# Streaming encoder layer on one core: gated activations held in PSUM until they are split, and up-weight sums placed between the down accumulations

## Chip, core and metric

The kernel runs on one core of a Trainium2 chip. The metric is the device time of one launch in microseconds (us), as the median of several runs. Engines are named as in the profile: PE is TensorE's matmul, PEld its weight load, DVE VectorE, ACT ScalarE, POOL GpSimd, SP the engine that issues the loads.

## What is computed

One layer of a hybrid encoder: an input projection, a pooling mixer beside grouped-query attention, an output projection with a residual, and a gated feed-forward block over 2048 + 64 rows of 1024 channels, with 2816 hidden channels. The change touches the last block alone:

```python
h = x + jnp.concatenate([pool_o, attn_o], axis=-1) @ w_out
hn = rms_norm(h, norm_ffn)
return h + (jax.nn.silu(hn @ w_gate) * (hn @ w_up)) @ w_down
```

## The kernel before

The rows go through the kernel in three parts (`Shape`, p = 0, 1, 2) of 768, 768 and 576 rows; the last part ends in the 64 sample rows. Each part runs projection, attention, output projection and then the feed-forward block, so there are three feed-forward stages.

**Precision.** Each fp32 operand is split into a high and a low fp32r half. `split_products` (L787) then makes three matmuls of one product (hi x hi, hi x lo, lo x hi: L790 to L792). ACT writes the high halves (`high_product`, L1226), POOL or DVE subtracts to get the low halves (POOL: L637).

**A feed-forward stage** is a loop over 11 groups of 256 hidden channels (j = 0 to 10). A group has a gate half (which = 0) and an up half (which = 1). Each half is a 2x2 block product made with seven block products instead of eight: `product` (L1052) issues them in the order 1, 6, 5, 7, 2, 3, 4 (`ORDER`). One product is 12 matmuls of 384 columns (288 in the third part). Between the two halves PE runs `down` of the group before (L1090), which multiplies its activations with `w_down`, tile by tile, and DVE adds each result to `h` (L1660). So PE's order in group j is: gate half of j, down of j-1, up half of j.

**Weight sums.** Products 5, 6 and 7 use sums of weight blocks, product 3 a further one. DVE makes them: `weight_sum(s, j, which, n)`, n = 1 to 4 (L1910, L1913, L1915, L1919). A ring of 4 slots holds the split weights: product q + 4 is split once product q is done.

**Block sums.** The seven products land in four PSUM banks: product 1 and 2 in bank 4, 6 in bank 5, 5 and 3 in bank 6, 7 and 4 in bank 7 (banks 0, 1, 2, 3 and 7 in group 0). `first_partial` (ACT, L1455) copies product 1 to `u2`, and DVE's `sums` combines: U2 (L1935), t (L1938), C22 (L1941), C12 (L1943), C21 (L1945). Gate sums go to `sg` in SBUF, up sums to `cc` and `u2` in SBUF. Product 4 accumulates onto product 7's bank, so PE waits for `c22_done` before it; a bank is written anew once the sum that read it is done.

**Activation.** ACT takes SiLU of the gate blocks (L1469). `gated` (DVE, L1963) multiplies an up block onto `sg`. ACT's `act_high` (L1476) rounds the result to `act_hi`, and DVE's `act_low` (L1975, and L1973 for the sample rows) subtracts to get `act_lo`. In the third part one `act_low` is three instructions. The last block's `act_high` and `act_low` run in the next group. `down_low` (DVE, L2019) makes the low half of the second `w_down` block, at the end of the group.

Every engine runs its instructions in written order and waits on semaphores, so what stands behind a waiting instruction waits too. DVE's order is the function `group` (L1979), ACT's the function `group` at L1479.

## Time and profile before

| what | value |
|---|---|
| median of 3 runs | 2350.99 us (2348.12 to 2352.45) |
| the profiled execution's own time | 2353.13 us |
| its span | 2351.3 us |
| PE busy | 2162.0 us, 92% |
| PEld busy | 1913.4 us, 81% |
| DVE busy | 1521.3 us, 65% |
| ACT busy, POOL busy | 939.1 us, 40%; 959.4 us, 41% |
| mean granted TensorE clock | 0.983 |
| chain that ended last | PE 59%, DVE 24%, issue 10%, ACT 6% |
| DMA | 160.04 MB, mean 68 GB/s |

The profile records one execution, whose own time lies 2.1 us above the median of the runs. Busy time of PE is modelled: a matmul's record is longer than the distance to the next one, since matmuls overlap. Distances between starts tell what one costs. The feed-forward stages run from about 285 to 808 us, 1101 to 1624 us and 1873 to 2331 us of the span.

### The profile page before, as it was taken

How to read it: one execution, taken by the hardware profiler on the slowest of the kernel's cores; microseconds unless marked ns; L12 is line 12 of the kernel's file. 1: busy time of each engine (PE TensorE's matmuls, PEld its weight loads, DVE VectorE, ACT ScalarE, POOL GpSimd, SP SyncE). 2: the span in 40 equal slices, each digit the busy share in tenths (PEclk: the TensorE clock that was granted, in tenths of full speed). 3: DMA queues.
4: the chain of work that ended last, by engine and by line, in shares of the span. 5: the costliest groups of instructions: out<-in, count | busy, mean ns of one | idle time of the engine just before them, and what ended most of it. 6: DMA issues, size and time to landing. Idle time of an engine off the chain costs nothing.

```text
span 2351.3 us, 34387 instructions
## 1 busy us (share of the span) xinstructions
PE 2162.0 (92%) x11991; PEld 1913.4 (81%) x11991; DVE 1521.3 (65%) x2375; ACT 939.1 (40%) x2070; POOL 959.4 (41%) x626
## 2 busy tenths in 40 slices
PE   7999899999999999998999999999998889898997
PEld 7876799988899788667999889988975678787886
DVE  4558665666666545675667665666458777777776
ACT  4666333332233346644333322324466333333331
POOL 2312354544454323123555434542311555555452
PEclk9999999999999999999999999999999999999999
DMA  4120022221122241110222212222411122222121
GB/s 132 45 71 29 11 90 68 68 80 54 54 71 67 87 143 55 54 37 19 72 72 73 70 54 62 68 67 83 143 33 58 40 90 81 80 71 84 58 81 50
DMA packets 194387, 160.04 MB, mean 68 GB/s; under 512 B 7005, under 2 KB 176906, under 8 KB 194282
## 3 DMA queue, kind: packets, MB, share of 16 engines
q1 hardware_dynamic: 191326, 149.58, 20.9%
q10 hardware_dynamic: 2956, 9.08, 1.1%
q8 instruction: 64, 1.05, 0.2%
q14 instruction: 41, 0.34, 0.0%
HBM read 149.66 MB, written 9.07 MB: 68 GB/s over the span
## 4 chain that ended last, share of the span: by engine, by line
PE 59%; DVE 24%; issue 10%; ACT 6%; DMA 0%; DVEq 0%; POOL 0%; SPq 0%; ACTq 0%
PE ps L790 18%; PE ps L791 18%; PE ps L792 18%; DVE act_lo L1975 5%; DVE s_sb L1819 2%; DVE negmax L1824 2%; ACT s_sb L1360 2%; DVE raw L1915 2%; DVE st L1910 2%; DVE sg L1963 1%; PE ps L804 1%; PE ps L897 1%; DVE h L1660 1%; DVE st L1919 1%; PE ps L935 1%
## 5 line engine op out<-in xcount | busy, mean ns | idle before, releaser
L637 POOL TENSOR_TENSOR ring_lo<-raw,ring_hi 128x512 fp32r<-128x512 f32 (+1 forms) x276 | 425.4, 1548 | 657.9 <-ACT ring_hi L1226 588.7
L1660 DVE TENSOR_TENSOR h<-ps,h 128x512 f32<-128x512 f32 (+1 forms) x476 | 325.4, 689 | 246.9 <-PE ps L792 237.2
L790 PE MATMUL ps<-xt_hi,ring_hi 128*128 128x384 f32 (+1 forms) x1152 | 380.1, 330 | 28.5 <-POOL ring_lo L637 24.4
L791 PE MATMUL ps<-xt_lo,ring_hi 128*128 128x384 f32 (+1 forms) x1152 | 376.3, 327 | 0.0
L792 PE MATMUL ps<-xt_hi,ring_lo 128*128 128x384 f32 (+1 forms) x1152 | 375.9, 326 | 0.0
L637 POOL TENSOR_TENSOR ring_lo<-st,ring_hi 128x512 fp32r<-128x512 f32 x198 | 265.3, 1347 | 178.5 <-ACT ring_hi L1226 178.1
L790 PE MATMUL ps<-tx,ring_hi 128*128 128x384 f32 (+1 forms) x792 | 259.6, 328 | 66.9 <-DVE sg L1941 61.2
L637 POOL TENSOR_TENSOR w_lo<-raw,w_hi 128x1024 fp32r<-128x1024 f32 x66 | 167.7, 2542 | 318.7 <-ACT w_hi L1203 318.6
L790 PE MATMUL ps<-w_hi,act_hi 128*128 128x512 f32 x704 | 284.3, 404 | 12.4 <-DVE act_lo L1975 9.9
L791 PE MATMUL ps<-w_lo,act_hi 128*128 128x512 f32 x704 | 282.7, 402 | 0.0
L792 PE MATMUL ps<-w_hi,act_lo 128*128 128x512 f32 x704 | 282.6, 401 | 0.0
L792 PE MATMUL ps<-tx,ring_lo 128*128 128x384 f32 (+1 forms) x792 | 256.8, 324 | 0.0
L791 PE MATMUL ps<-tx,ring_hi 128*128 128x384 f32 (+1 forms) x792 | 256.8, 324 | 0.0
L1455 ACT ACTIVATE uu<-ps 128x384 f32<-128x384 f32 (+1 forms) x66 | 30.7, 465 | 561.7 <-PE ps L792 498.1
L790 PEld LDWEIGHTS ps<-xt_hi,ring_hi 128*128 128x128 f32 x1152 | 218.7, 190 | 36.0 <-POOL ring_lo L637 16.1
L791 PEld LDWEIGHTS ps<-xt_lo,ring_hi 128*128 128x128 f32 x1152 | 218.7, 190 | 1.4
L792 PEld LDWEIGHTS ps<-xt_hi,ring_lo 128*128 128x128 f32 x1152 | 218.6, 190 | 0.0
L790 PEld LDWEIGHTS ps<-tx,ring_hi 128*128 128x128 f32 x792 | 150.1, 189 | 77.0 <-issue 69.3
L1226 ACT ACTIVATE ring_hi<-raw 128x512 fp32r<-128x512 f32 x264 | 162.3, 626 | 98.3 <-PE ps L792 96.2
L1226 ACT ACTIVATE ring_hi<-st 128x512 fp32r<-128x512 f32 x198 | 124.2, 629 | 163.2 <-DVE st L1919 88.6
L790 PEld LDWEIGHTS ps<-w_hi,act_hi 128*128 128x128 f32 x704 | 135.7, 193 | 45.2 <-issue 12.4
L792 PEld LDWEIGHTS ps<-w_hi,act_lo 128*128 128x128 f32 x704 | 134.9, 192 | 33.2
(206 smaller groups left out, 4225.0 us busy)
## 6 DMA issues: line engine op xcount, KB each, us to landing
raw<-in_w_gate SPq DMA_DIRECT2D x66, 512.0 KB, 4.4
raw<-in_w_up SPq DMA_DIRECT2D x66, 512.0 KB, 4.0
raw<-in_w_down SPq DMA_DIRECT2D x66, 512.0 KB, 3.3
raw<-in_w_in SPq DMA_DIRECT2D x33, 512.0 KB, 4.0
raw<-in_w_out SPq DMA_DIRECT2D x24, 512.0 KB, 4.4
h<-in_x_prompt SPq DMA_DIRECT2D x16, 512.0 KB, 6.9
out<-h ACTq DMA_DIRECT2D x16, 512.0 KB, 2.8
xload<-in_x_prompt SPq DMA_DIRECT2D x10, 512.0 KB, 6.0
```

The costliest lines, as they stand in the source:

```text
L637: nc.gpsimd.tensor_tensor(lo, raw, hi.bitcast(F32), ALU.subtract).then_inc(done, 1)
L790: nc.tensor.matmul(out, w_hi, m_hi, start=first, stop=False, skip_group_check=onto)
L791: nc.tensor.matmul(out, w_hi, m_lo, start=False, stop=False, skip_group_check=onto)
L792: return nc.tensor.matmul(out, w_lo, m_hi, start=False, stop=last, skip_group_check=onto)
L1226: nc.scalar.activation(ring_hi[:, slot], left(which, p), ACT.Copy).then_inc(hi_done, 1)
L1360: nc.scalar.activation(p, p, ACT.Exp, bias=negmax[0:rows, ai % 2, hh:hh + 1], accum_out=den[0:rows, ai % 2, hh:hh + 1])
L1660: nc.vector.tensor_tensor(out, ps[0:rows, bank, :], out, ALU.add).then_inc(d_free, 1)
L1819: last = nc.vector.scalar_tensor_tensor(s_sb[0:rows, b, hh, c0:c1], dist[0:rows, c0:c1], SLOPES[GQA * g + hh], ps[0:rows, 4 + e, 256 * j + ...
L1824: link(nc.vector.tensor_reduce(negmax[0:rows, b, :], s_sb[0:rows, b, :, c0:c1], AX.X, ALU.max, negate=True))
L1910: nc.vector.tensor_tensor(first, b[:, 0:HALF], b[:, HALF:], ALU.add).then_inc(s_ready, 1)
L1915: nc.vector.tensor_tensor(b[:, 0:HALF], a[:, 0:HALF], b[:, 0:HALF], ALU.subtract)\
L1975: last = nc.vector.tensor_tensor(act_lo[:, c, dst], sg[:, b, src], act_hi[:, c, dst].bitcast(F32), ALU.subtract)
```

## The change

Four things change; the number of compute instructions stays.

- **Where the up sums and the product live.** The up half's C22, C12 and C21 are written back to PSUM: C22 to the bank of U2's product, C12 and C21 to the bank that they read. `gated` multiplies in place in PSUM, by `sg` from SBUF. `act_high` and `act_low` read PSUM. `a_bank` names the banks.
- **Who waits for that.** PE's first gate product of the next group waits for `al_done` of the second block where it waited for `a_done`; products 5 and 7 of the gate half get a wait for the third and the fourth block's `al_done`. `first_partial` of the gate half no longer waits for the last `gated`.
- **DVE's order.** The four up sums of weights leave the place between t and C22 of the gate half: n = 1 goes behind C21, n = 2 and 3 behind the first tile's accumulation, n = 4 behind the third tile's. The sums of the next gate half move up by one tile. `down_low` of j-1 moves from the end of group j-1 to between t and C22 of the gate half of j. The last `act_low` goes from the next group to the end of its own.
- **ACT's order.** The last `act_high` goes from the next group to its own, ahead of the second `w_down` rounding (L1502).

```diff
+        def a_bank(j, block):
+            first = isinstance(j, int) and j == 0
+            b = BLOCKS.index(block)
+            return ps[:, ((2, 1, 3, 7) if first else (5, 4, 6, 7))[b]]
...
                 if p == 1 and not first:
                     if which == 0:
-                        pe.wait_ge(a_done, s.g0 + 4 * j - 2)
+                        pe.wait_ge(al_done, s.g0 + 4 * j - 2)
...
                 elif p == 5:
                     need(pe, c12_done, m)
+                    if which == 0 and not first:
+                        pe.wait_ge(al_done, s.g0 + 4 * j - 1)
                 elif p == 7:
                     need(pe, c21_done, m)
+                    if which == 0 and not first:
+                        pe.wait_ge(al_done, s.g0 + 4 * j)
...
                     if s and prev and 1 <= t <= s.nt:
+                        if t == 1:
+                            pe.wait_ge(al_done, prev.g0 + 4 * GROUPS)
                         norm_transposes(s, t - 1)
...
-                if which == 0:
-                    need(act, a_done, s.g0 + 4 * j)
-                else:
-                    act.wait_ge(c21_done, m)
+                need(act, c21_done, m)
...
-                    need(act, al_done, s.g0 + 4 * j - 2)
+                    need(act, a_done, s.g0 + 4 * j - 2)
...
-                    last = nc.scalar.activation(act_hi[:, c, dst], sg[:, b, src], ACT.Copy)
+                    last = nc.scalar.activation(act_hi[:, c, dst], a_bank(j, block)[:, src], ACT.Copy)
...
-                    if n == 0:
-                        act_high(s, j - 1, (1, 0))
+                    if p == 4 and which == 1:
+                        act_high(s, j, (1, 0))
...
-                out = cc[:, 0:s.NB] if which else sg[:, BLOCKS.index(block), 0:s.NB]
+                out = sg[:, BLOCKS.index(block), 0:s.NB]
+                if which:
+                    out = cc[:, 0:s.NB] if part in ("U2", "t") else a_bank(j, block)[:, 0:s.NB]
+                t_tile = cc[:, 0:s.NB] if which else out
...
-                g = sg[:, b, 0:s.NB]
-                nc.vector.tensor_tensor(g, up, g, ALU.mult).then_inc(a_done, 1)
+                up = a_bank(j, block)[:, 0:s.NB]
+                nc.vector.tensor_tensor(up, up, sg[:, b, 0:s.NB], ALU.mult).then_inc(a_done, 1)
...
-                    last = nc.vector.tensor_tensor(act_lo[:, c, dst], sg[:, b, src],
+                    last = nc.vector.tensor_tensor(act_lo[:, c, dst], a_bank(j, block)[:, src],
                                                    act_hi[:, c, dst].bitcast(F32), ALU.subtract)
...
                 weight_sum(s, j, 0, 4)
-                if not first:
-                    act_low(s, j - 1, (1, 0))
                 sums(s, j, 0, "U2")
                 sums(s, j, 0, "t")
-                for n in (1, 2, 3):
-                    weight_sum(s, j, 1, n)
+                if first:
+                    for n in (1, 2, 3):
+                        weight_sum(s, j, 1, n)
+                else:
+                    down_low(s, j - 1)
                 for part in ("C22", "C12", "C21"):
                     sums(s, j, 0, part)
+                if not first:
+                    weight_sum(s, j, 1, 1)
+                between = {0: () if first else ((1, 2), (1, 3)), 1: ((0, 1),), 2: ((0, 2), (1, 4)), 3: ((0, 3),)}
                 for t in range(s.nt):
                     if not first:
                         accumulate_tile(s, OUT_GROUPS + j - 1, odd, t, t)
-                    if 1 <= t <= 3 and not last:
-                        weight_sum(s, j + 1, 0, t)
-                weight_sum(s, j, 1, 4)
+                    for which, n in between.get(t, ()):
+                        if which == 1:
+                            weight_sum(s, j, 1, n)
+                        elif not last:
+                            weight_sum(s, j + 1, 0, n)
...
                 act_low(s, j, (0, 1))
-                if last:
-                    act_low(s, j, (1, 0))
-                else:
-                    down_low(s, j)
+                act_low(s, j, (1, 0))
```

DVE at the start of a group (j = 9 of the first part, whose instructions stand unrolled), before: the last weight sum of the gate half (L1919), the `act_low` that was left over, U2, t, three up sums of weights, then the three block sums.

```order
L1919 TENSOR_TENSOR st<-raw,st 128x512 [waits split2]
L1975 TENSOR_TENSOR act_lo<-sg,act_hi 128x384 [waits ah_done]
L1935 TENSOR_TENSOR uu<-ps,uu 128x384 [waits u1_done,prod_done]
L1938 TENSOR_TENSOR sg<-ps,uu 128x384 [waits u2_done,prod_done]
L1910 TENSOR_TENSOR st<-raw 128x512 [waits split2,raw2_loaded3,raw2_loaded2]
L1913 TENSOR_TENSOR st<-st,raw 128x512 [waits s_ready]
L1915 TENSOR_TENSOR raw<-raw 128x512
L1941 TENSOR_TENSOR sg<-ps,sg 128x384 [waits t_done,prod_done]
L1943 TENSOR_TENSOR sg<-ps,uu 128x384 [waits prod_done]
L1945 TENSOR_TENSOR sg<-ps,uu 128x384 [waits prod_done]
L1660 TENSOR_TENSOR h<-ps,h 128x512 [waits d_ready] x4
```

The same place in the changed kernel (its lines stand 6 to 12 lower in the file: L1928 is L1919 before, L2028 is L2019, L1953 is L1941, L1669 is L1660).

```order
L1928 TENSOR_TENSOR st<-raw,st 128x512 [waits split2]
L1947 TENSOR_TENSOR uu<-ps,uu 128x384 [waits u1_done,prod_done]
L1950 TENSOR_TENSOR sg<-ps,uu 128x384 [waits u2_done,prod_done]
L2028 TENSOR_TENSOR w_lo<-raw,w_hi 128x1024 [waits hi_done]
L1953 TENSOR_TENSOR sg<-ps,sg 128x384 [waits t_done,prod_done]
L1955 TENSOR_TENSOR sg<-ps,uu 128x384 [waits prod_done]
L1957 TENSOR_TENSOR sg<-ps,uu 128x384 [waits prod_done]
L1919 TENSOR_TENSOR st<-raw 128x512 [waits split2,raw2_loaded3,raw2_loaded2]
L1669 TENSOR_TENSOR h<-ps,h 128x512 [waits d_ready] x2
L1922 TENSOR_TENSOR st<-st,raw 128x512 [waits s_ready]
L1924 TENSOR_TENSOR raw<-raw 128x512
L1669 TENSOR_TENSOR h<-ps,h 128x512 [waits d_ready] x2
```

Between t and C22 one instruction now stands where three stood, and the three up sums stand behind C21 and the first tile.

DVE at the end of the same group, from the up half's C22 on, before, up to the first instruction of the next group:

```order
L1941 TENSOR_TENSOR uu<-ps,uu 128x384 [waits t_done,prod_done]
L1963 TENSOR_TENSOR sg<-uu,sg 128x384 [waits c22_done,silu_done]
L1963 TENSOR_TENSOR sg<-ps,sg 128x384 [waits prod_done,silu_done]
L1975 TENSOR_TENSOR act_lo<-sg,act_hi 128x384 [waits ah_done]
L1943 TENSOR_TENSOR uu<-ps,uu 128x384 [waits prod_done]
L1963 TENSOR_TENSOR sg<-uu,sg 128x384 [waits c12_done,silu_done]
L1975 TENSOR_TENSOR act_lo<-sg,act_hi 128x384 [waits ah_done]
L1945 TENSOR_TENSOR uu<-ps,uu 128x384 [waits prod_done]
L1963 TENSOR_TENSOR sg<-uu,sg 128x384 [waits c21_done,silu_done]
L1975 TENSOR_TENSOR act_lo<-sg,act_hi 128x384 [waits ah_done]
L2019 TENSOR_TENSOR w_lo<-raw,w_hi 128x1024 [waits hi_done]
L1919 TENSOR_TENSOR st<-raw,st 128x512 [waits split2]
```

In the changed kernel:

```order
L1953 TENSOR_TENSOR ps<-ps,uu 128x384 [waits t_done,prod_done]
L1969 TENSOR_TENSOR ps<-ps,sg 128x384 [waits c22_done,silu_done]
L1969 TENSOR_TENSOR ps<-ps,sg 128x384 [waits prod_done,silu_done]
L1981 TENSOR_TENSOR act_lo<-ps,act_hi 128x384 [waits ah_done]
L1955 TENSOR_TENSOR ps<-ps,uu 128x384 [waits prod_done]
L1969 TENSOR_TENSOR ps<-ps,sg 128x384 [waits c12_done,silu_done]
L1981 TENSOR_TENSOR act_lo<-ps,act_hi 128x384 [waits ah_done]
L1957 TENSOR_TENSOR ps<-ps,uu 128x384 [waits prod_done]
L1969 TENSOR_TENSOR ps<-ps,sg 128x384 [waits c21_done,silu_done]
L1981 TENSOR_TENSOR act_lo<-ps,act_hi 128x384 [waits ah_done] x2
L1928 TENSOR_TENSOR st<-raw,st 128x512 [waits split2]
```

Every instruction but the last now reads or writes PSUM for the activations, `w_lo` is gone from the end, and a fourth `act_lo` stands there.

## Rows read from the trace of the kernel before

**Rows 1.** PE's waits: who waited for what, us in total, times, longest.

```profile
PE ps L790 <- DVE sg L1941: 61.2, 31, 2.5
PE ps L790 <- POOL ring_lo L637: 24.4, 24, 1.5
...
PE ps L790 <- DVE act_lo L1975: 9.9, 3, 4.4
```

**Rows 2.** Windows of one group: bounds, length, busy per engine, PEclk, DMA share, GB/s.

```profile
478.06:526.35 48.29, 46.53 (x240) 42.93 (x241) 30.93 (x40) 14.56 (x27) 22.70 (x15) 1.00 0.22 65
1964.40:2007.40 43.00, 37.89 (x225) 33.98 (x225) 31.43 (x48) 14.13 (x31) 22.16 (x15) 0.96 0.24 74
2007.40:2048.85 41.45, 36.35 (x224) 32.70 (x225) 31.39 (x48) 14.04 (x31) 22.18 (x15) 1.00 0.25 76
```

**Rows 3.** Timeline of PE, first part: start, length, instruction, [idle before <- releaser].

```profile
524.08 0.34 PE L791 MATMUL ps<-xt_lo,ring_hi 128*128 128x384 f32 x1
524.25 0.34 PE L792 MATMUL ps<-xt_hi,ring_lo 128*128 128x384 f32 x1
526.35 0.41 PE L790 MATMUL ps<-tx,ring_hi 128*128 128x384 f32 x1 [1.77 <-DVE sg L1941]
...
560.07 0.34 PE L790 MATMUL ps<-xt_hi,ring_hi 128*128 128x384 f32 x1
```

**Rows 4.** Timeline of DVE, same gate half.

```profile
521.27 1.08 DVE L1910 TENSOR_TENSOR st<-raw 128x512 f32<-128x512 f32 x1
...
523.98 1.76 DVE L1915 TENSOR_TENSOR raw<-raw 128x512 f32<-128x512 f32 x1
525.66 0.54 DVE L1941 TENSOR_TENSOR sg<-ps,sg 128x384 f32<-128x384 f32 x1
```

**Rows 5.** Timeline of POOL, the same gate half and the up half behind it.

```profile
521.76 3.43 POOL L637 TENSOR_TENSOR ring_lo<-raw,ring_hi 128x512 fp32r<-128x512 f32 x2
...
558.98 1.59 POOL L637 TENSOR_TENSOR ring_lo<-st,ring_hi 128x512 fp32r<-128x512 f32 x1 [0.73 <-ACT ring_hi L1226]
```

**Rows 6.** By line: instructions, ns min/median/max, first and last start, forms.

```profile
L1935 DVE TENSOR_TENSOR uu<-ps,uu x66: 443/547/558, 297.7 to 2318.8; 128x384 f32<-128x384 f32 x44, 128x288 f32<-128x288 f32 x22
L1963 DVE TENSOR_TENSOR sg<-uu,sg x99: 458/559/2548, 313.1 to 2329.8; 128x384 f32<-128x384 f32 x66, 128x288 f32<-128x288 f32 x33
L2019 DVE TENSOR_TENSOR w_lo<-raw,w_hi x33: 1217/2307/2310, 323.6 to 2326.7; 128x1024 fp32r<-128x1024 f32 x33
```

**Rows 7.** Timeline of DVE, end of an up half.

```profile
558.19 0.56 DVE L1943 TENSOR_TENSOR uu<-ps,uu 128x384 f32<-128x384 f32 x1 [1.09 <-PE ps L792]
558.85 0.56 DVE L1963 TENSOR_TENSOR sg<-uu,sg 128x384 f32<-128x384 f32 x1
559.33 1.66 DVE L1975 TENSOR_TENSOR act_lo<-sg,act_hi 128x384 fp32r<-128x384 f32 x1
```

**Rows 8.** Timeline of PE, a gate half of the third part.

```profile
1991.81 0.30 PE L790 MATMUL ps<-xt_hi,ring_hi 128*128 128x288 f32 x1
1991.94 0.29 PE L791 MATMUL ps<-xt_lo,ring_hi 128*128 128x288 f32 x1
...
1997.18 0.37 PE L790 MATMUL ps<-tx,ring_hi 128*128 128x288 f32 x1 [0.44 <-DVE uu L1945]
...
2000.53 0.39 PE L790 MATMUL ps<-xt_hi,ring_hi 128*128 128x288 f32 x1 [1.52 <-POOL ring_lo L637]
...
2003.03 0.40 PE L790 MATMUL ps<-xt_hi,ring_hi 128*128 128x288 f32 x1 [0.65 <-POOL ring_lo L637]
...
2007.39 0.37 PE L790 MATMUL ps<-tx,ring_hi 128*128 128x288 f32 x1 [2.50 <-DVE sg L1941]
```

**Rows 9.** Timeline of DVE, the same place.

```profile
1992.75 2.63 DVE L1975 TENSOR_TENSOR act_lo<-sg,act_hi 128x256 fp32r<-128x256 f32 x1
```

**Rows 10.** Timeline of ACT, the same place.

```profile
1997.63 0.41 ACT L1455 ACTIVATE uu<-ps 128x288 f32<-128x288 f32 x1 [2.77 <-DVE sg L1963]
```

**Rows 11.** Timeline of PE behind a wait in the first part's last group.

```profile
719.95 0.52 PE L791 MATMUL ps<-tx,ring_hi 128*128 128x384 f32 x1
```

More of the change, by code:

```diff
@@ L1505, in group @@
                         silu(s, j, block)
-                    elif block and (p != 4 or last):
+                    elif block and p != 4:
                         act_high(s, j, block)
@@ L1940, in sums @@
                     dve.wait_ge(t_done, m + 1)
-                    nc.vector.tensor_tensor(out, b4, out, ALU.add).then_inc(c22_done, 1)
+                    nc.vector.tensor_tensor(out, b4, t_tile, ALU.add).then_inc(c22_done, 1)
                 elif part == "C12":
@@ L1944, in sums @@
                 else:
-                    nc.vector.tensor_tensor(two if which else out, b4, two, ALU.add).then_inc(c21_done, 1)
+                    nc.vector.tensor_tensor(out, b4, two, ALU.add).then_inc(c21_done, 1)
             def gated(s, j, block):
-                first = isinstance(j, int) and j == 0
                 m, b = s.m0 + 2 * j + 1, BLOCKS.index(block)
@@ L1954, in gated @@
                     dve.wait_ge(prod_done, s.q0 + seq(j, 1, 2) + 1)
[L1955 to L1963 removed]
+                else:
+                    dve.wait_ge({(1, 1): c22_done, (0, 1): c12_done, (1, 0): c21_done}[block], m + 1)
+                up = a_bank(j, block)[:, 0:s.NB]
+                nc.vector.tensor_tensor(up, up, sg[:, b, 0:s.NB], ALU.mult).then_inc(a_done, 1)
             def act_low(s, j, block):
```

10 lines of the change are left out of this document (2 added, 8 removed).

## The prediction

> **What bounds the kernel now.** I read the waits of PE first, since PE is busy for 92% of the span. One wait outweighs all others: product 4's first matmul waits for C22 of the gate half, 31 times, 61.2 us together; behind it come 24 waits for POOL's low halves, 24.4 us [rows 1]. Then the windows of single groups: in the first two parts a group takes 48.3 us, in the third 41.5 us, or 43.0 us where the granted clock reads 0.96 [rows 2]. So the thing to read is one group, and what PE waits for in it.
>
> In the first two parts PE's matmuls of a product start 0.17 us apart; before product 4 of the gate half 2.10 us pass between two starts [rows 3]. That costs 1.93 us, once in each of groups 1 to 10. DVE shows why: product 7 is long done, but three up sums of weights stand between t and C22, from 521.27 to 525.66, 4.4 us [rows 4]. Two of them are slow: 1.08 and 1.76 us. POOL is in its own subtractions just then, two of them in 3.43 us [rows 5]. C22 ends at 526.20 and PE starts at 526.35: 0.15 us from the end of a DVE instruction to the matmul that waits for it.
>
> In the third part four waits stand in one gate half: 0.44 us for C21 of the up half before, 1.52 and 0.65 us for POOL's low halves, 2.50 us for C22 [rows 8]. Starts are 0.13 us apart and a record is 0.30 us, so each wait costs its idle time plus 0.17 us: 5.11 + 0.68 = 5.8 us per group, in ten groups. The cause lies before them: `act_low` of an up block takes 2.63 us [rows 9], the last `gated` comes late behind it, and ACT's `first_partial` waits 2.77 us for that [rows 10]. ACT's rounding of product 2's weights stands behind `first_partial`, and POOL's low half behind that.
>
> **DVE's slow instructions.** The record shows when they are slow. A sum with one operand in PSUM and one in SBUF never exceeds 558 ns over 66 instructions, in the same stretches in which POOL works. `gated` with both operands in SBUF has the same median, 559 ns, but reaches 2548 ns; the `w_down` subtraction takes 1217 ns at least and 2307 ns in the median [rows 6]. The `act_low` of 1.66 us [rows 7] starts 0.35 us after a POOL subtraction of 1.59 us [rows 5].
>
> **The change, part by part.**
>
> *Up sums out of the gate half.* The three sums, 4.4 us, leave the stretch between t and C22. `down_low` takes their place. It is unhidden only if it delays C22. Its ends are 1.22 and 2.31 us [rows 6]; I take the upper, since POOL has four subtractions to make there. Count from gate product 1's start (time 0), a product being 2.1 us: U2 can start at about 4.3, t at 6.4, `down_low` ends by 9.3. C22 needs product 7, done at 8.4, so it ends at about 9.8; product 4 begins at 12.6. There are 2.8 us to spare and the wait goes. Saving: 1.93 us x 20 groups = 38.6 us in the first two parts. Below zero this cannot fall, unless something else becomes late (next items).
>
> *Where the sums go.* Behind C21 and between the down accumulations. DVE is busy for 30.9 of 48.3 us [rows 2], and its idle time lies mostly between the accumulations of `down`, whose 16.9 us (13.1 in the third part; a group less its 14 products and waits) need no new ring slot. Four sums of 0.7 us (1.8 if POOL interferes) are 2.8 to 7.2 us; the accumulations may fall behind by one unit, since PE runs four banks ahead. ACT is held before the split of product 6's weights until sum 2 is done, 3.4 to 5 us into `down`; three splits and POOL's three low halves (1.3 to 1.6 us each) end 9 to 10 us into it. PE wants them at 13.1 at the earliest. I cost this at zero; what covers it is `down`.
>
> *Activations in PSUM.* No operand pair lies in SBUF any more, so `gated` and `act_low` should take 0.56 us, or 0.46 in the third part [rows 6]. No row shows DVE writing PSUM. Its nearest rows are 0.56 us, the sums that read it, and 2.55 us, the worst of these places in SBUF; nothing suggests less than 0.56, as the element count is the same. I take 0.56, whose rows have the same operands. The gain is that C21 and the last `gated` come on time and that `first_partial` follows C21.
>
> *The new wait.* PE's first gate product now waits for `act_low` of the second block. The chain is: C12 at 558.19, `gated` at 558.85, `act_low` at 559.33 [rows 7]. At 0.56 us it ends at 559.89, plus 0.15 is 560.04; PE starts that product at 560.07 [rows 3]. It just fits: I allow 0.1 us x 20 = 2 us. In the third part C12 starts 1.4 us ahead of product 1's due start, `gated` 0.56 later, `act_low` 0.37 after that, and its three pieces end 0.6 us on: 0.15 us past the due start, with the 0.15 of the release 0.3 to 0.4 us a group. What queues behind it on PE is everything. Products 5 and 7 wait for blocks three and four, due at 1.9 and 2.8 us, when PE needs them at 4.2 and 6.3 (3.2 and 4.8 in the third part): nothing. ACT's last `act_high` goes ahead of one 1.05 us rounding and behind one `gated`; `first_partial` still comes at about 3 us instead of 3.6.
>
> The Trainium skill, "VectorE: DVE Perf Modes", section on the TRN2 errata, gives a PSUM source 62 cycles more fixed cost than an SBUF source. By it, as an estimate, two instructions of this chain would be 0.065 us longer each, and the sum 30 x 0.13 = 4 us higher. The medians of 547 and 559 ns [rows 6] show no such difference, so I leave it out.
>
> *Third part.* Without the late `gated`, product 2's low half is done at about 6.2 us, before PE needs it (6.8). Product 3's is tight: weight sum 4 and `down_low` alternate with POOL's subtractions, which puts it at 8.7, when PE wants it at 8.2: 0.4 us. Product 4's comes at 10.0, due at 10.4. So of 5.8 us some 0.8 stay: 5.0 x 10 = 50 us.
>
> *Ends of the parts.* The last `down` of each part waits for `act_low`, 9.9 us in the three, 4.4 us in the last [rows 1]. There `gated` of the first block waits out POOL's `w_down` subtraction, with up to 2.55 us [rows 6]. At 0.56 or 0.46 us it ends 1.5 to 2.1 us earlier, of which ACT's roundings and the products themselves let 1.0 to 2.0 through: 4 us together.
>
> *TensorE's clock.* Seven times in the loops the spacing is that of 1.2 GHz for some 3 us, a matmul reading 0.52 us [rows 11] against 0.34 [rows 3]; each time it begins within 1.4 us after a wait of 1.8 us or more. In the third part that is the difference of 43.00 and 41.45, 1.55 us [rows 2]; the seven cost 10.8 us. With no wait over 0.5 us left in the loops they should go; I take 9 us.
>
> **Sum:** 38.6 - 2 + 50 + 4 + 9 = 99.6 us. The profiled execution took 2353.1 us, which gives 2253.5; the median of the runs lies 2.1 us lower, so **2251 us**. All of the 38.6, 58 and 10.8 us and the 9.9 us of the part ends together would be 117 us, 2234: no time below that.
>
> **Rivals.**
>
> *POOL holds the third part.* The 1.52 and 0.65 us waits need not hang on `first_partial`. For it: POOL is busy 22.2 of 41.5 us [rows 2], nearly all of it in the two halves and the first of `down`. Against: it idles before product 2. If both stay, 2.5 us a group instead of 0.4 are 21 us: 2272. A DVE write to PSUM of 0.8 us instead of 0.56 adds 0.5 us at product 1, 30 times, up to 2287.
>
> *DVE stays slow.* If an instruction that writes PSUM still has to take turns with POOL, `act_low` of the second block ends at 560.99 as before [rows 7] and product 1 waits 1.1 us in 20 groups; in the third part it ends 4.8 us late. Then 20 x 0.8 + 10 x 1 us remain of the gains in the loops, with some clock: 2320.
>
> *Slower.* The wait at product 1 takes the place of that at product 4 and is longer. Place: DVE's `act_low` of block 2. POOL's `w_down` subtraction starts about 0.2 us after time 0; if `act_low` falls behind it, as its 2.63 us show [rows 9], it ends near 3.4 and PE waits 3.6 us in place of 1.93. The point from which it decides is 1.8 us past product 1's due start. 20 x 1.6 us = 32 us: 2383. Against: operands in PSUM have never waited for POOL.
>
> *No effect.* The savings in the gate half return as waits in the up half, because ACT stands behind weight sum 2. That needs it some 7 us later than worked out above: 2350.
>
> **Chances.** Forecast 0.66, own range 2238 to 2266; POOL or a dearer PSUM write 0.25, 2266 to 2290; DVE slow 0.04; slower 0.03; no effect 0.02. The range 2238 to 2288 leaves out under 2 in 10. About 0.2%, 5 us, is what can be told from no change here. Faster: 0.95; the same: 0.02; slower: 0.03.
>
> **What would show it.** Right: a group of 46.4 us in the first two parts and 36.5 in the third; no PE wait for C22; `gated` and `act_low` with a maximum near 560 ns; a small wait of PE for `act_lo` at product 1; no loop window with a clock under 0.99. Wrong: `act_lo` as PE's largest releaser with more than 0.5 us a time; POOL's low half before products 2 and 3 of the third part; DVE instructions `ps<-ps,sg` over 0.8 us.

## The result, and the profile after

The changed kernel takes **2237.9 us** in the median of four runs (2237.53 to 2238.54), the kernel before beside it 2351.7 us: ratio 0.9515, with a 95% interval of 0.9497 to 0.9533. The forecast was 2251 us with a range from 2238 to 2288; the result lies a tenth of a microsecond under the low end, some 13 us below the forecast.

| what | before | after |
|---|---|---|
| the profiled execution's own time | 2353.13 us | 2238.25 us |
| its span | 2351.3 us | 2236.4 us |
| PE busy | 92% | 95% |
| DVE busy | 1521.3 us, 65% | 1327.4 us, 59% |
| ACT, POOL busy | 939.1, 959.4 us | 938.4, 940.2 us |
| mean granted TensorE clock | 0.983 | 0.990 |
| chain that ended last | PE 59%, DVE 24%, issue 10% | PE 80%, DVE 11%, ACT 6% |

From the start of group 0's second product to the first matmul of the last `down`, a stage's length went as follows. Stages one and two: 522.8 to 499.8 us and 522.4 to 499.8 us, together 45.6 us less. Stage three: 457.5 to 392.4 us, 65.1 us less. Everything outside these stretches: 4.2 us less. The forecast's sum, sorted in the same way (its clock term by the places of the seven stretches, its part ends by part), had about 43, 57 and 0.

First PE's waits in the changed kernel, the answer to [rows 1]; columns are who waited for whom, us in total, times, longest.

```profile
PE ps L796 <- DVE act_lo L1981: 6.5, 5, 2.3
PE ps L796 <- POOL ring_lo L643: 3.1, 6, 0.9
...
PE ps L796 <- DVE sg L1953: 0.7, 1, 0.7
```

The 31 waits for C22 are down to one, in group 0 of the third part; the 24 for POOL's low halves to six. What is left for `act_lo` are the three ends of the parts and two short ones, at product 1 of the last two of the third part's ten groups; in the other eight PE is idle there for 0.07 us, too little to be counted. The windows of single groups, which answer to [rows 2], one of the first part and one of the third (bounds, length, busy of PE, PEld, DVE, ACT, POOL with counts, PEclk, DMA share, GB/s):

```profile
499.96:546.22 46.26, 46.26 (x242) 42.94 (x241) 25.89 (x39) 14.60 (x26) 21.85 (x16) 1.00 0.23 68
...
2052.69:2088.50 35.81, 35.74 (x225) 32.63 (x225) 24.28 (x49) 13.96 (x31) 22.05 (x16) 1.00 0.30 88
```

In the first part PE is busy for all of the 46.26 us: nothing but its own products is left. The third part is at 35.81 us with 0.07 us idle. DVE, which makes 2375 instructions in either kernel, is busy for 5.0 us less per group in the first part, and 7.1 us less in the third (31.39 before).

By line, the answer to [rows 6]: instructions, ns min/median/max, first and last start, forms.

```profile
L1953 DVE TENSOR_TENSOR ps<-ps,uu x33: 466/566/567, 315.5 to 2209.0; 128x384 f32<-128x384 f32 x22, 128x288 f32<-128x288 f32 x11
...
L1969 DVE TENSOR_TENSOR ps<-ps,sg x132: 456/567/567, 316.2 to 2214.8; 128x384 f32<-128x384 f32 x88, 128x288 f32<-128x288 f32 x44
...
L1981 DVE TENSOR_TENSOR act_lo<-ps,act_hi x176: 181/487/558, 318.2 to 2216.3; 128x384 fp32r<-128x384 f32 x88, 128x256 fp32r<-128x256 f32 x44, 128x32 fp32r<-128x32 f32 x44
...
L2028 DVE TENSOR_TENSOR w_lo<-raw,w_hi x33: 1215/1215/1434, 328.6 to 2211.6; 128x1024 fp32r<-128x1024 f32 x33
```

The maximum of `gated` fell from 2548 to 567 ns, that of `act_low` to 558. Here a write of 384 columns to PSUM costs 9 ns more than one to SBUF (567 against 558 ns). And `down_low`, priced at 2.31 us in the forecast, takes 1.2 us in its new place in the first two parts, 1.35 to 1.43 us in the third. Gate product 4 of the first part shows why it may now stand there, against [rows 3, 4]. DVE first, then PE; columns are start, length, instruction.

```profile
559.96 1.22 DVE L2028 TENSOR_TENSOR w_lo<-raw,w_hi 128x1024 fp32r<-128x1024 f32 x1
561.57 0.56 DVE L1953 TENSOR_TENSOR sg<-ps,sg 128x384 f32<-128x384 f32 x1 [0.40 <-PE ps L798]
```

```profile
565.43 0.34 PE L798 MATMUL ps<-xt_hi,ring_lo 128*128 128x384 f32 x1
565.61 0.34 PE L796 MATMUL ps<-tx,ring_hi 128*128 128x384 f32 x1
```

C22 ends at 562.12, 3.3 us before PE wants it, and starts are 0.18 us apart across the boundary. The new dependence at product 1, in the first part, against [rows 7]:

```profile
551.77 0.57 DVE L1969 TENSOR_TENSOR ps<-ps,sg 128x384 f32<-128x384 f32 x1
552.25 0.55 DVE L1981 TENSOR_TENSOR act_lo<-ps,act_hi 128x384 fp32r<-128x384 f32 x1
```

```profile
552.81 0.34 PE L798 MATMUL ps<-tx,ring_lo 128*128 128x384 f32 x1
552.99 0.34 PE L796 MATMUL ps<-xt_hi,ring_hi 128*128 128x384 f32 x1
```

`act_low` ends at 552.80, and PE starts at 552.99 without a gap. How near that is depends on the release: C22's end and the matmul that waits for it are 0.15 us apart [rows 3, 4], but where PE does wait for `act_low` at product 1, it starts 0.06 us after its end in the first eight of a part's ten groups and 0.15 us after it in the last two (the third part here, all parts in `e6_act_low_twice` below). So in this group, the sixth, the step has 0.14 us to spare; in the last two it has 0.05. In the third part the same step is late, and product 3 just so. DVE, PE and POOL of one group there:

```profile
2141.57 0.41 DVE L1981 TENSOR_TENSOR act_lo<-ps,act_hi 128x256 fp32r<-128x256 f32 x1
...
2147.75 1.35 DVE L2028 TENSOR_TENSOR w_lo<-raw,w_hi 128x1024 fp32r<-128x1024 f32 x1
```

```profile
2142.32 0.37 PE L796 MATMUL ps<-xt_hi,ring_hi 128*128 128x288 f32 x1 [0.16 <-DVE act_lo L1981]
...
2150.34 0.38 PE L796 MATMUL ps<-xt_hi,ring_hi 128*128 128x288 f32 x1
2150.55 0.30 PE L797 MATMUL ps<-xt_lo,ring_hi 128*128 128x288 f32 x1
```

```profile
2147.97 2.29 POOL L643 TENSOR_TENSOR ring_lo<-st,ring_hi 128x512 fp32r<-128x512 f32 x1
```

At product 1 the distances between starts are 0.40 us longer than they would be (0.32 before the first matmul, 0.08 before the second), at product 3 0.08 us (2150.34 to 2150.55 instead of 0.13). This is the ninth of the ten groups; in the seven before it, with the shorter release, product 1 costs 0.34 us (0.23 and 0.11) and product 3 0.15 us (0.04 and 0.11). The four waits of [rows 8] are gone, but for 0.58 and 0.48 us for POOL's low halves in the first of the ten. Note that an idle time under 0.1 us has no bracket in the timeline: the distance between starts is the surer reading.

### The profile page after: what moved, and what is told of

It is laid out like the page before. It is cut to its first block, busy times and chain, and to the rows that moved or that the text cites. A ratio compares the mean times of both kernels' runs of the same rounds, so it can differ in the third digit from the quotient of the medians.

```text
span 2236.4 us, 34415 instructions
## 1 busy us (share of the span) xinstructions
PE 2135.8 (95%) x11991; PEld 1900.1 (85%) x11991; DVE 1327.4 (59%) x2375; ACT 938.4 (42%) x2070; POOL 940.2 (42%) x626
## 3 DMA queue, kind: packets, MB, share of 16 engines
q8 instruction: 64, 1.05, 0.2%
## 4 chain that ended last, share of the span: by engine, by line
PE 80%; DVE 11%; ACT 6%; issue 2%; POOL 1%; DMA 1%; SPq 0%; DVEq 0%; ACTq 0%; POOLq 0%
PE ps L796 25%; PE ps L797 25%; PE ps L798 25%; DVE s_sb L1828 2%; DVE negmax L1833 2%; ACT s_sb L1372 2%; PE ps L810 1%; PE ps L903 1%; DVE h L1669 1%; PE ps L941 1%; DVE xt_lo L1876 1%; PE ps L919 1%; DVE kt_sb L1750 1%; ACT pt_sb L1389 1%; POOL ring_lo L643 1%
## 5 line engine op out<-in xcount | busy, mean ns | idle before, releaser
L643 POOL TENSOR_TENSOR ring_lo<-raw,ring_hi 128x512 fp32r<-128x512 f32 (+1 forms) x276 | 414.3, 1509 | 438.6 <-ACT ring_hi L1238 373.3
L1669 DVE TENSOR_TENSOR h<-ps,h 128x512 f32<-128x512 f32 (+1 forms) x476 | 322.0, 686 | 148.9 <-PE ps L798 145.1
L643 POOL TENSOR_TENSOR w_lo<-raw,w_hi 128x1024 fp32r<-128x1024 f32 x66 | 159.4, 2417 | 318.6 <-ACT w_hi L1215 318.6
L796 PE MATMUL ps<-tx,ring_hi 128*128 128x384 f32 (+1 forms) x792 | 254.6, 321 | 1.3 <-DVE sg L1953 0.7
L797 PE MATMUL ps<-tx,ring_hi 128*128 128x384 f32 (+1 forms) x792 | 254.3, 321 | 0.0
L797 PEld LDWEIGHTS ps<-w_lo,act_hi 128*128 128x128 f32 x704 | 133.0, 189 | 30.6
```

What stands on the lines that cost most here:

```text
L643: nc.gpsimd.tensor_tensor(lo, raw, hi.bitcast(F32), ALU.subtract).then_inc(done, 1)
L796: nc.tensor.matmul(out, w_hi, m_hi, start=first, stop=False, skip_group_check=onto)
L797: nc.tensor.matmul(out, w_hi, m_lo, start=False, stop=False, skip_group_check=onto)
L1669: nc.vector.tensor_tensor(out, ps[0:rows, bank, :], out, ALU.add).then_inc(d_free, 1)
```

## The experiments

The table gives the length of a group in the steady stretch of each kind of part, and the median.

| kernel | parts 1 and 2 | part 3 | median, us |
|---|---|---|---|
| before | 48.29 | 41.45 | 2351.7 |
| new order alone | 46.30 | 38.29 | 2274.4 |
| PSUM alone | 46.91 | 37.33 | 2266.9 |
| changed, but product in SBUF | 47.04 | 40.37 | 2293.4 |
| changed, `down_low` at the end | 46.27 | 36.24 | 2245.5 |
| changed | 46.26 | 35.81 | 2237.9 |

### Each half of the change alone

`e1_psum_alone` keeps the activations in PSUM and goes back to DVE's order of before, but for the last `act_low`, which stays at the end of its own group:

```diff
-                else:
-                    down_low(s, j - 1)
...
+                for n in (1, 2, 3):
+                    weight_sum(s, j, 1, n)
...
+                if not last:
+                    down_low(s, j)
```

> The changed kernel with the weight sums and the w_down subtraction back in their old places; only the activations stay in PSUM (and the last act_low stays at the end of its group). Theory A (each half of the change is enough for the wait at product 4 in the first two parts): with gated and act_low at 0.56 us, DVE reaches t about 3.3 us earlier than before, the three sums still stand ahead of C22, but C22 ends at about 11.1 us after gate product 1's start where PE needs it at 12.4: no wait, a group of 46.3 us. In the third part PE needs it at 9.9 and a wait of about 1 us stays: 37 us a group, 2250 us in all. Theory B (as the prediction had it: the place of the sums makes the wait at product 4): the wait of 1.8 us stays in most of the 20 groups and that of 2.5 us in the third part's ten, 20 x 1.9 + 10 x 2.7 = 65 us over the changed kernel, 2303 us.

Measured: 2266.9 us (ratio 0.9639, 0.9623 to 0.9656), between the two. Theory A was right for the third part (37.33 us a group, 37 expected) and wrong for the first two (46.91 us in place of 46.3); Theory B put the wait three to five times too long. The waits of PE, and DVE's gate half in this kernel:

```profile
PE ps L796 <- DVE sg L1953: 16.9, 31, 0.8
```

```profile
518.75 1.53 DVE L1919 TENSOR_TENSOR st<-raw 128x512 f32<-128x512 f32 x1
520.32 1.67 DVE L1922 TENSOR_TENSOR st<-st,raw 128x512 f32<-128x512 f32 x1
521.91 1.77 DVE L1924 TENSOR_TENSOR raw<-raw 128x512 f32<-128x512 f32 x1
523.61 0.54 DVE L1953 TENSOR_TENSOR sg<-ps,sg 128x384 f32<-128x384 f32 x1
```

The wait for C22 is back at all 31 places, but with 0.4 us in the first part and 0.83 us in the third, not 1.77 and 2.50. The three sums are as slow as ever (4.9 us from the first one's start to C22's, 4.4 before); the gate half's work merely begins earlier. The prediction put the wait at product 4 down to the place of the sums alone, but 1.38 of its 2.0 us in the first parts go without touching that place.

`e2_order_alone` is the kernel before with the new places of DVE's sums and of `down_low` and nothing else; its last `act_low` still runs in the next group:

```diff
-                for n in (1, 2, 3):
-                    weight_sum(s, j, 1, n)
+                if first:
+                    for n in (1, 2, 3):
+                        weight_sum(s, j, 1, n)
+                else:
+                    down_low(s, j - 1)
```

> The kernel before with the new order of DVE alone: sums between the down accumulations, w_down's subtraction between t and C22; activations in SBUF as before. Both theories: the wait for C22 goes in all three parts. Theory A and B alike give 46.3 us a group in the first two parts. In the third part the waits for C21 (0.44 us) and for POOL's low halves (1.52 and 0.65 us), which I put down to the late gated and act_low, stay: about 3 us a group, 39 us a group, low-clock stretches fewer than before: 2275 us. If the POOL waits came from the sums instead, this kernel would reach the changed one's 35.8 us a group and 2245 us.

Measured: 2274.4 us (0.9672, 0.9651 to 0.9693). In parts one and two the order alone does the whole thing, 1.99 of 2.02 us a group. In the third it leaves 2.5 us a group (L1938 is the sum t, L1945 C21):

```profile
PE ps L790 <- POOL ring_lo L637: 11.4, 13, 1.0
PE ps L790 <- DVE sg L1938: 11.1, 10, 1.8
...
PE ps L790 <- DVE uu L1945: 5.7, 10, 1.9
```

The wait for t is new. It stands at product 3, where the kernel before waited for POOL's low half, and is 11.1 us in the ten groups; the forecast of 2275 us was met with this wait in the place of one of POOL's that it had named.

So the two halves, order and PSUM, save 77 and 85 us alone and 114 together. They overlap: each shortens the same queue of DVE in front of the same matmuls, and what one has freed the other can't free again.

### What matters about PSUM

`e3_product_in_sbuf` is the changed kernel whose `gated` writes the product to SBUF; ACT's rounding and `act_low` read it there. ACT's SiLU of the next gate half, which writes the same buffer, must then wait for `act_low`. The line that matters most:

```diff
-                nc.vector.tensor_tensor(up, up, sg[:, b, 0:s.NB], ALU.mult).then_inc(a_done, 1)
+                nc.vector.tensor_tensor(sg[:, b, 0:s.NB], up, sg[:, b, 0:s.NB], ALU.mult).then_inc(a_done, 1)
```

> The changed kernel, but gated writes its product to sg in SBUF, and act_high and act_low read it there; the up sums stay in PSUM, PE's waits stay as changed. Theory L (an instruction of DVE with both operands in SBUF takes turns with POOL, one with an operand in PSUM doesn't): gated stays at 0.56 us, act_low reads up to 1.6 to 2.6 us again, PE waits for the second block's act_low 1.1 us in each of 20 groups and 3.5 to 4.8 us in each of the third part's ten: 2295 to 2310 us. Theory W (what made gated and act_low slow before was their late start behind the sums, not their operands): act_low stays near 0.56 us and the time within 5 us of the changed kernel's 2238.

Measured: 2293.4 us (0.9752, 0.9731 to 0.9772), just under the range of Theory L and 50 us from Theory W: product 1 comes 0.77 us late in the first two parts, where 1.1 was expected. `gated` stays fast (one input in PSUM, 558 ns); `act_low`, both inputs now in SBUF, has a mean of 1221 ns for the shape that took 551. The third part shows it at its plainest, on DVE, POOL and PE:

```profile
1985.80 1.41 DVE L1981 TENSOR_TENSOR act_lo<-sg,act_hi 128x256 fp32r<-128x256 f32 x1
1987.13 2.32 DVE L1979 TENSOR_TENSOR act_hi<-sg,act_hi 128x32 fp32r<-128x32 f32 x1
```

```profile
1986.89 2.52 POOL L643 TENSOR_TENSOR w_lo<-raw,w_hi 128x1024 fp32r<-128x1024 f32 x1
```

```profile
1989.62 0.40 PE L796 MATMUL ps<-xt_hi,ring_hi 128*128 128x288 f32 x1 [3.21 <-DVE act_lo L1981]
```

An instruction over 32 columns, 0.18 us elsewhere, takes 2.32 us and ends at 1989.45, when POOL's subtraction ends (1989.41). This is the mechanism that the rival "slower" had put at this place, with 3.6 us of waiting: 3.21 us were measured once the input lay in SBUF. The Trainium skill, "SBUF — State Buffer", section "Who interferes with whom", says that a DVE instruction with two SBUF inputs contends with a GpSimd instruction that reads SBUF and that one with at most one, outside the two-port modes, does not. All rows above agree: of the 132 `gated` and 176 `act_low` of the changed kernel none exceeds 567 ns.

### What `down_low` is worth in the gate half

`e4_down_low_at_end` moves it back to the end of the group.

```diff
-                else:
-                    down_low(s, j - 1)
...
+                if not last:
+                    down_low(s, j)
```

> The changed kernel with the w_down subtraction of DVE back at the end of its group instead of between t and C22. If its place matters (as the prediction cost it, 2.3 us in turns with POOL there, and 0.4 us of wait at product 3 in the third part), the third part gets 0.3 us a group faster or, as it now meets POOL's 2.4 us w_down subtraction, U2 and t come 1 us later, still ahead of PE. My theory: DVE has 2.8 us to spare in the gate half either way, the time stays within 3 us of 2238. The rival, that this place was needed: waits of PE for u2 or t, over 0.3 us a group, 2247 us or more.

Measured: 2245.5 us (0.9543, 0.9527 to 0.9559). The forecast of this run, no more than 3 us, was wrong: the third part's group is 36.24 us, 0.43 us longer, and the whole third stage 3.4 us. PE's timeline of one such group has it at product 7:

```profile
2010.68 0.40 PE L796 MATMUL ps<-tx,ring_hi 128*128 128x288 f32 x1 [0.16 <-POOL ring_lo L643]
```

The start before it is at 2010.22, so that product 7 comes 0.33 us late and its second matmul another 0.10. Product 2 is 0.14 us late too, while product 3, 0.15 us late in the changed kernel, is on time. Of the 8.8 us between the two profiled runs 3.4 are these; 2.4 lie ahead of the first stage and 3.0 between the first two, where the granted clock shows more stretches at 1.2 GHz (at 238, 269 and 1061 us) than in the changed kernel's profile. Nothing was changed there, so they are not put down to the move.

`e7_down_low_twice` makes the subtraction twice where the change has put it.

```diff
+                if not last:
+                    nc.vector.tensor_tensor(w1_lo[:, 1], raw1[:, 1], w1_hi[:, 1].bitcast(F32), ALU.subtract)\
+                        .then_inc(dose, 1)
+                    dve.wait_ge(dose, (GROUPS - 1) * s.p + j + 1)
```

> The changed kernel with down_low's subtraction made twice in the gate half (1.2 to 1.35 us, with a 0.1 us turn between). It tests the step of the prediction that gave product 3 of the third part 0.4 us of waiting behind POOL. Theory: POOL's low half for product 3 ends at the moment PE wants it (2150.26 against 2150.34 plus the release), and with one more two-input subtraction in SBUF on DVE it ends about 1.2 us later, in ten groups: 12 us, 2250 (2246 to 2253); the first two parts keep 46.27 us, since C22 has 3.3 us there. Rival: POOL is not held by DVE but only DVE by POOL, and nothing changes in the third part either: 2238 to 2240.

Measured: 2248.8 us (2243.9 to 2250.2; 0.9555, 0.9541 to 0.957). Parts one and two keep 46.27 us. The third part's group is 36.42 us, 0.61 longer, half of what was expected, and at another product. That the median falls into the expected 2246 to 2253 us is luck: the profiled run took 2243.9 us, 5.6 us over the changed kernel, and the longer times of the others are not in what the profile shows.

```profile
2078.66 1.43 DVE L2030 TENSOR_TENSOR w_lo<-raw,w_hi 128x1024 fp32r<-128x1024 f32 x1
2080.12 2.20 DVE L2033 TENSOR_TENSOR w_lo<-raw,w_hi 128x1024 fp32r<-128x1024 f32 x1
```

```profile
2078.97 2.27 POOL L644 TENSOR_TENSOR ring_lo<-st,ring_hi 128x512 fp32r<-128x512 f32 x1
2081.20 3.51 POOL L644 TENSOR_TENSOR ring_lo<-raw,ring_hi 128x512 fp32r<-128x512 f32 x2
```

```profile
2083.51 0.40 PE L797 MATMUL ps<-tx,ring_hi 128*128 128x288 f32 x1 [0.36 <-POOL ring_lo L644]
```

In these rows DVE and POOL take turns instruction by instruction, each ending 1.1 to 1.2 us after the other. The low half of product 3 pays for the first copy only; the second copy delays the one of product 4 by about that much. Product 4 starts 0.52 us late, so it had some 0.6 us to spare.

### How tight product 1 is

`e6_act_low_twice` puts one more subtraction ahead of the `act_low` for which product 1 waits.

```diff
+                if b == 1:
+                    src, dst = s.pieces(nb)[0]
+                    nc.vector.tensor_tensor(cc[:, src], a_bank(j, block)[:, src],
+                                            act_hi[:, c, dst].bitcast(F32), ALU.subtract)
```

> The changed kernel with one more subtraction of the same size into a scratch buffer just ahead of act_low of block (0,0), the one that PE's first gate product waits for. My theory: in the first two parts act_low ends just as PE gets there (552.80 plus 0.15, PE at 552.99), so the 0.47 us of one more instruction show as 0.43 us in 20 groups, and in the third part, which already waits, as 0.33 us in 10 groups: 12 us more, 2250 (2247 to 2254). Rival: there is slack that the profile does not show (the wait is covered by PE's queue), and only the third part pays: 2241.

Measured: 2247.4 us (2242.0 to 2252.4; 0.9544, 0.9525 to 0.9563). A group takes 46.69 us in the first two parts, 0.43 more, and 36.02 in the third, 0.21 more. PE at product 1 of the first part:

```profile
556.32 0.34 PE L798 MATMUL ps<-tx,ring_lo 128*128 128x384 f32 x1
556.82 0.44 PE L796 MATMUL ps<-xt_hi,ring_hi 128*128 128x384 f32 x1 [0.16 <-DVE act_lo L1985]
557.10 0.34 PE L797 MATMUL ps<-xt_lo,ring_hi 128*128 128x384 f32 x1
```

The 0.43 us are those worked out, but by luck. The first start is late by 0.33 us only, and the second by another 0.11, which the working left out; `act_low` ends 0.06 us ahead of PE's start, not 0.15, in all but the last two groups of a part. So of the 0.46 us that `act_low` comes later 0.33 show, and the slack in these groups is 0.14 us: little, but more than the 0.04 that a release of 0.15 us gives. In the third part product 1 pays the expected 0.33 us, and the 0.12 us that product 3 lost before are gone behind it.

### What sends the clock down

`e8_wait_dose` brings the wait at product 4 back by repeated sums whose result goes to a scratch buffer, 7, 9 and 11 of them in the three parts.

```diff
+                        for i in range(n):
+                            nc.vector.tensor_tensor(cc[:, 0:s.NB], b4, t_tile, ALU.add).then_inc(dose, 1)
+                            dve.wait_ge(dose, base + i + 1)
```

> The changed kernel with sums repeated into a scratch buffer ahead of C22 of the gate half, so that PE waits before product 4 again in groups 1 to 10: 7 sums in the first part, 9 in the second, 11 in the third, which by the trace (C22's end at 562.12, product 4 at 565.6; 0.66 us a repeated sum, 0.56 in the third part) makes the wait about 1.35, 2.7 and 3.7 us. It tests what sends the clock to 1.2 GHz. Theory: the low stretches follow waits of about 1.8 us or more, so none in the loops of the first part, some (2 to 5) in the second, most groups in the third, about 1.6 us each: 77.5 us of waits and 8 to 20 us of clock, 2323 to 2336. Rival: the stretches come by chance and have nothing to do with the waits: 2315, and no more low stretches than the changed kernel has.

Measured: 2312.6 us (2307.1 to 2316.2; 0.983, 0.9815 to 0.9845). The repeated sums came out shorter than assumed. PE's product 4 in the three parts:

```profile
569.66 0.41 PE L798 MATMUL ps<-tx,ring_hi 128*128 128x384 f32 x1 [0.64 <-DVE sg L1961]
...
1276.84 0.41 PE L798 MATMUL ps<-tx,ring_hi 128*128 128x384 f32 x1 [1.83 <-DVE sg L1961]
...
2055.89 0.37 PE L798 MATMUL ps<-tx,ring_hi 128*128 128x288 f32 x1 [2.85 <-DVE sg L1961]
```

The idle times are the same to 0.01 us in the groups of a part, 0.64, 1.83 and 2.85 us, but for the third part's first wait of 2.12 us. Behind them a stretch of 3.0 to 3.4 us in which starts lie as far apart as at 1.2 GHz follows after none of the ten in the first part, after four of the ten in the second (at 1131, 1278, 1425 and 1571 us), after seven of the nine long ones in the third. Each costs 1.5 to 1.7 us. The four of the second part come at every third group, 147 us apart. The time alone would not have told the theories apart, because the waits added 60 us, not 77; the count of stretches does: eleven where the changed kernel has none.

### Trying to go further

`e5_early_low` brings `act_low` of block (0, 0) ahead of the sum C12, and in the last group two of them ahead of C21.

```diff
+                else:
+                    act_low(s, j, (0, 0))
                 sums(s, j, 1, "C12")
```

> The changed kernel with act_low of the first block moved ahead of the sum C12 in all groups but the last, and in the last group act_low of the first two blocks ahead of the sum C21. My theory: DVE's order alone makes the 0.33 us at product 1 of the third part (ten groups, 3.3 us), since block (0,0) is rounded long before C12 and its low half only waits behind it, and about 1.5 us of the 2 us wait at each of the three part ends, because there the low halves stand behind C21: 7 to 8 us in all, so 2230 us (2228 to 2233), with the third part's group at 35.5 us instead of 35.82. Rival: act_low then delays C12 and the gated product of block (0,1) by its own half microsecond, ACT's rounding of it comes later, and the wait only moves to product 5 or to ACT: 2238, no change.

Measured: 2237.1 us (2232.5 to 2240.8), ratio 0.9504 (0.9489 to 0.9519): no gain, and the rival was right that the wait only moves, though not in where it goes. Product 1 starts without a gap, and the third part's group still takes 35.82 us:

```profile
2112.29 0.40 PE L796 MATMUL ps<-tx,ring_hi 128*128 128x288 f32 x1
...
2115.70 0.40 PE L796 MATMUL ps<-xt_hi,ring_hi 128*128 128x288 f32 x1
```

The starts before these are at 2112.04 and 2115.44, so that 0.12 us are lost at product 7 and 0.13 at product 3, and 0.11 more behind each. Both take their low half from POOL. At the ends of the parts little of the expected 4.5 us was gained. From the first matmul of the tenth `down` to the next stage's first product 59.7 us pass in the first part, as in the changed kernel: PE's wait for `act_lo` of 1.95 us is gone, but 1.05 us of waiting for C21 stand in its place, and the wait ahead of the next stage's first product grows from 1.90 to 2.50 us. In the second part the same stretch is 0.7 us shorter (58.8 to 58.1), and in the third, up to the last instruction, 0.8 us (44.7, against 45.5 in the profiles that have no stretch at 1.2 GHz there). What the first two parts' groups lose (46.30 in place of 46.27 us) takes 0.6 of it back.

That pointed to two chains of equal length in the third part, DVE's and POOL's. `e9_pool_late` shortens POOL's: its subtraction of the down weights goes behind product 4's low half.

```diff
+                        if n == 2 and order is not GROUP0:
+                            low1(DOWN_ID, first - 2)
                         if n in down_at:
                             number = number + 1
-                            if n == down_at[0]:
+                            if n == down_at[0] and last:
```

> The changed kernel with POOL's subtraction of the down weights (2.4 us) moved from ahead of the low half of gate product 7 to behind that of gate product 4, where POOL has time before the down products. It asks what holds the third part's group at 35.82 us, 0.4 us over what its products alone take, since the run with the early act_low left it at 35.82. Theory: two chains are equally long there, DVE's act_low in front of product 1 and POOL's low halves for products 7 to 3; taking POOL's alone away frees 0.1 us at product 3 and leaves the 0.33 at product 1: 35.7 us a group, 1 us in all, 2237. Rival: POOL alone is the bound, and the whole 0.4 us goes: 35.4, 2234. Second rival: the load of the next down weights waits for this subtraction and the next gate weights' load stands behind it on SP's queue; then the weight sums between the accumulations come late: 2240 or more.

`e10_pool_late_early_low` adds to it the early `act_low` in the third part (but its last group), and the changed kernel itself ran beside them.

> Both at once: POOL's subtraction of the down weights behind gate product 4's low half, and, in the third part but its last group, act_low of block (0,0) ahead of the sum C12. Theory of the two equally long chains: the third part's group falls to the products' own time, 35.4 us, no start of PE in the gate half over 0.1 us late: 9 x 0.4 = 3.6 us under the changed kernel, 2234. Rival (a third chain, ACT's, lies just behind): 35.7 to 35.8 us, 2237 to 2238.

> The changed kernel itself, beside the two others on the same chip, since they are expected only 1 to 4 us away from it: 2238 (2236 to 2240) by both theories.

Measured: 2235.4 us (2232.1 to 2236.4) with POOL's move alone, **2232.4 us** (2232.3 to 2236.3; ratio 0.949, 0.9477 to 0.9503) with both, and 2239.1 us (2237.0 to 2240.5) for the changed kernel. A window of one group of the third part of each, first POOL's move alone, then both:

```profile
2081.86:2117.54 35.68, 35.62 (x226) 32.62 (x225) 22.68 (x47) 13.96 (x30) 21.22 (x16) 1.00 0.30 88
```

```profile
1972.39:2007.79 35.40, 35.40 (x227) 32.63 (x225) 23.28 (x47) 13.91 (x30) 21.27 (x16) 1.00 0.30 89
```

Neither move alone frees the group, 35.82 and 35.69 us; both do, 35.40 us with PE busy throughout. The group lengths account for 3.4 us of the 6.7 between the medians; the spans of the profiled runs differ by 4.6, the rest of which, 1.1 us, lies ahead of the third part's loop. For POOL's move alone the groups account for 1.1 us of 3.7. What is left of the medians' differences isn't explained, so the surer evidence for the two chains is the group lengths. With both moves it is the fastest version that was run, by its median.

## Why the prediction was right, and where it was off

*What bounds, and the wait for C22: right.* The wait at product 4 went in all 20 groups of the first two parts. The order alone takes 1.99 us off each, where 1.93 were forecast. The cause named, the place of the sums, was only part of it: with the sums in their old place and only `act_low` and `gated` fast, the wait shrinks from 1.77 to 0.40 us.

*Where the sums go, at zero: right.* ACT is idle for 9.3 us inside `down` until weight sum 2 is done, and no matmul waits for what stands behind it: group windows in the first parts are PE's own time.

*Activations in PSUM, 0.56 us: right.* It was 0.567 at most. The added cost for a PSUM source that the Trainium skill gives in "VectorE: DVE Perf Modes", in the section on the TRN2 errata, is not in these rows: `act_low` from PSUM takes 558 ns at most, the multiplication of two SBUF operands before took 559 in the median [rows 6]. The bound of 2.55 us at the other end was what the same instructions cost in SBUF, as the run with the product there shows.

*The new wait in the first parts, 0.1 us a group: too much.* It is zero, with 0.14 us to spare in eight of a part's ten groups, where the release from `act_low` takes 0.06 us and not the 0.15 of C22, and 0.05 us in the last two. That is 2 us.

*Third part, "of 5.8 us some 0.8 stay: 5.0 x 10 = 50 us": this is the step that failed.* The four waits cost 6.05 us a group before and leave 0.4 to 0.5 (35.81 us, against 35.40 with both further moves), so that 5.64 us went in place of 5.0: 6.4 us in ten groups. The mechanism held, and of its two remaining waits the one at product 1 measured 0.34 us, inside the 0.3 to 0.4 it was given, though by two errors that cancel: the release is 0.06 us and not 0.15 in eight of the ten groups, and the second start, 0.11 us late, was left out. Two sizes in the term were off. The first is product 3: 0.4 us forecast, 0.08 to 0.15 measured. The likely reason is `down_low`: it was priced at 2.31 us, its median in the old place, because POOL has four subtractions to make in the new one, and takes 1.35 there. That `down_low` is what holds product 3 is shown by the run with it at the end of the group, where product 3 is on time; that its price makes the whole difference no run shows. The second is what a wait costs before the change: idle time plus 0.17 us leaves out that the second start behind a wait is 0.08 to 0.11 us late too. With it the gaps between starts add up to 6.1 us a group in place of 5.8. The second could have been read beforehand, from the starts behind the waits of [rows 8], which the forecast did not look at; for the first it had the minimum of 1217 ns in [rows 6] as its lower end and did not take it.

*The clock, 9 of 10.8 us: right in kind, too small.* All seven stretches in the loops went. What the step left out lies outside the loops: stretches behind the waits at the ends of the parts and between the stages, some 4 us in the profile. Outside the three stages the profile before takes 848.6 us and the changed one 844.4, but those of the variants, which for the most part change nothing there, take from 839 to 850, so this part of the gain is not established by one profile; the runs of one kernel also differ by up to 10 us.

*The ends of the parts, 4 us: right.* The waits for `act_lo` in `down` fell from 9.9 us to 6.2.

*The floor of 2234 us* was drawn with the same omissions; 2232.4 us was reached with two more moves.

*The rivals.* POOL as the bound of the third part was true for its last 0.4 us only, and there not alone: POOL's chain and DVE's end together, and the two had to be shortened together. "DVE stays slow" and "slower" fell with the 567 ns maximum; with the product in SBUF the second one's mechanism appears at its place.

So the forecast for the profiled run, 2253.5 us, was 15 us high: 8.1 from the third part with its clock, 2.6 from the first two, 4.2 from outside these stages. The 8.1 are 6.4 from the groups and the rest from the clock and the stage's ends. All three errors have one sign, and the range's low end, set at the sum of the known waits with nothing for these, was too near.

## What to carry to other kernels

A DVE instruction over two SBUF operands may have to wait out the subtraction that POOL is making just then (2.32 us in place of 0.18, ending with POOL's); leaving one operand in PSUM brought the worst case of `gated` from 2548 to 567 ns, for 9 ns a write. When two repairs act on one queue, measure each alone: here 77 and 85 us gave 114. And when a wait that was taken away only moves, look for a second chain of the same length before giving up: in the third part's groups two moves worth nothing and 1.1 us alone were worth 3.4 us together.

## What had not been expected of the hardware

The granted clock fell behind waits of 1.83 us in four of ten cases, and of 2.85 us in seven of nine, with waits equal to 0.01 us; at 0.64 us it never did in ten. The kernel before shows the same: three of its 20 waits of 1.77 us were followed by a low stretch, and four of the ten of 2.50 us. So one wait is not like another of the same length. In the second part the low stretches come at every third group, which speaks for something regular and against pure chance; what it is no run here shows.

A 32-column subtraction took 2.32 us, thirteen times its usual 0.18, because it met a long one of POOL: short instructions are not spared.
